# The order of k tiles and output tiles within a weight chunk of a streaming encoder step

## The reference

```
h = rms_norm(x, attn_norm[i])
y, state = even_mixer(h, ...) if i % 2 == 0 else odd_mixer(h, ...)   # h @ w_in, two attentions, concat @ w_out
x = x + y
h = rms_norm(x, mlp_norm[i])
x = x + square(relu(h @ w_up[i])) @ w_down[i]
```

## Time and profile before

| | |
|---|---|
| time, median of 3 runs | 2524.15 us (2524.02 to 2524.26) |
| span of the profiled execution, first to last instruction | 2521.4 us |
| TensorE busy, matmuls | 2514.2 us, 19,196 matmuls |
| VectorE busy | 1356.5 us |
| ScalarE busy | 998.4 us |
| DMA | 439.10 MB, mean 174 GB/s |
| granted TensorE clock, mean | 1.000 |

### The profile page before, as it was taken

One profiled execution on the slowest core, in us unless ns is written; L12 is line 12 of the kernel. 1 busy time (PEld: TensorE's weight loads), 2 busy tenths in 40 slices (PEclk: granted clock), 3 DMA queues, 4 the chain that ended last, 5 costly groups with the idle time before them and its releaser, 6 DMA issues.

```text
span 2521.4 us, 46114 instructions
## 1 busy us (share of the span) xinstructions
PE 2514.2 (100%) x19196; PEld 2487.2 (99%) x19196; DVE 1356.5 (54%) x1647; ACT 998.4 (40%) x1285; POOL 63.4 (3%) x104
## 2 busy tenths in 40 slices
PE   9999999999999999999999999999999999999999
PEld 9999999999999999999999999999999999999999
DVE  6487776544554454455544564765544544544543
ACT  5344445333333333334433455453333333333332
POOL 0002120000000000000000000000000000000000
PEclk9999999999999999999999999999999999999999
DMA  6554665444444444444444556544444444444454
GB/s 238 180 186 163 217 195 201 160 167 167 167 166 163 166 167 167 168 167 164 163 167 167 180 178 210 207 168 167 166 164 166 166 167 167 167 164 165 165 181 149
DMA packets 118525, 439.10 MB, mean 174 GB/s; under 512 B 14051, under 2 KB 14309, under 8 KB 116037
## 3 DMA queue, kind: packets, MB, share of 16 engines
q1 hardware_dynamic: 109728, 398.77, 45.3%
q0 software_dynamic: 6304, 30.94, 3.6%
q10 hardware_dynamic: 2308, 6.64, 0.9%
HBM read 426.04 MB, written 10.19 MB: 173 GB/s over the span
## 4 chain that ended last, share of the span: by engine, by line
PE 99%; DVE 0%; DMA 0%; issue 0%; ACT 0%; DVEq 0%; ACTq 0%; POOLq 0%
PE ps L425 29%; PE ps L427 29%; PE ps L426 28%; PE ps L391 3%; PE ps L393 3%; PE ps L392 3%; PE ps L579 1%; PE ps L622 1%; PE ps L453 0%; PE ps L455 0%; PE ps L454 0%; PE ps L623 0%; PE ps L525 0%; PE ps L637 0%; PE ps L774 0%; PE ps L593 0%
## 5 line engine op out<-in xcount | busy, mean ns | idle before, releaser
L839 ACT CAST w_high<-raw 128x1024 fp32r<-128x1024 f32 x755 | 787.0, 1045 | 942.4 <-PE ps L427 916.4
L1206 DVE TENSOR_TENSOR w_low<-raw,w_high 128x1024 fp32r<-128x1024 f32 x755 | 906.5, 1217 | 448.9 <-ACT w_high L839 425.5
L425 PE MATMUL ps<-x_parts,w_high 128*128 128x288 f32 x3408 | 1012.7, 297 | 0.0
L426 PE MATMUL ps<-x_parts,w_high 128*128 128x288 f32 x3408 | 1002.6, 294 | 0.0
L427 PE MATMUL ps<-x_parts,w_low 128*128 128x288 f32 x3408 | 1001.2, 294 | 0.0
L426 PEld LDWEIGHTS ps<-x_parts,w_high 128*128 128x128 f32 x3408 | 643.3, 189 | 0.2
L425 PEld LDWEIGHTS ps<-x_parts,w_high 128*128 128x128 f32 x3408 | 638.2, 187 | 5.4 <-issue 3.3
L427 PEld LDWEIGHTS ps<-x_parts,w_low 128*128 128x128 f32 x3408 | 642.5, 189 | 0.0
L425 PE MATMUL ps<-hid_parts_a,w_high 128*128 128x288 f32 x1024 | 302.3, 295 | 0.0
L426 PE MATMUL ps<-hid_low_b,w_high 128*128 128x288 f32 x1024 | 302.3, 295 | 0.0
L427 PE MATMUL ps<-hid_high_b,w_low 128*128 128x288 f32 x1024 | 302.3, 295 | 0.0
(11 more groups left out here) (330 smaller groups left out, 1818.5 us busy)
## 6 DMA issues: line engine op xcount, KB each, us to landing
raw<-in_w SPq DMA_DIRECT2D x755, 512.0 KB, 3.2
tmp<-norm_rows ACTq DMA_DIRECT2D x6, 576.0 KB, 4.3
proj<-norm_rows ACTq DMA_DIRECT2D x4, 576.0 KB, 5.0
scr<-in_k_past_B POOLq DMA_DIRECT2D x2, 1024.0 KB, 5.5
scr<-in_v_past_B POOLq DMA_DIRECT2D x2, 1024.0 KB, 7.5
scr<-in_k_past_C POOLq DMA_DIRECT2D x2, 1024.0 KB, 6.4
scr<-in_v_past_C POOLq DMA_DIRECT2D x2, 1024.0 KB, 8.3
scr<-in_k_past_D POOLq DMA_DIRECT2D x2, 1024.0 KB, 5.2
```

The lines of the kernel that those rows point to most:

```text
L425: pe.matmul(out, wh, high, start=k == 0, stop=end and apart)
L426: pe.matmul(out_low, wh, low, start=k == 0 and apart, stop=False)
L839: act.copy(used(n, w_high[:, c % HB, :]), used(n, raw[:, c % RB, :])).then_inc(high_ready, 1)
L1206: dve.tensor_tensor(used(n, w_low[:, c % RB, :]), used(n, raw[:, c % RB, :]), used(n, w_high[:, c % HB, :]).bitcast(F32), ALU.subtract)\
```

## The change

Within a chunk the loops over k tiles and output tiles change places, in both functions that hold the large products. The matmuls, their slices, their operands and their number stay. Only the order of the eight triples is another. `start` and `stop`, which mark the first and last matmul of an accumulation, still go by k.

```diff
@@ out_pair
-                    for k2 in range(CK):
-                        k = 8 * half + CK * i + k2
-                        high, low = HID(k)
-                        for f in range(GF):
+                    for f in range(GF):
+                        for k2 in range(CK):
+                            k = 8 * half + CK * i + k2
+                            high, low = HID(k)
                             at = (k2 * GF + f) * P
                             out = ps[:, 2 * (e % 2) + f, 0:T]
                             wh = w_high[:, c % HB, at:at + P]
@@ group
-                    for k2 in range(CK):
-                        k = kk * CK + k2
-                        high, low = moving(k)
-                        for f in range(tiles):
+                    for f in range(tiles):
+                        for k2 in range(CK):
+                            k = kk * CK + k2
+                            high, low = moving(k)
                             at = (k2 * GF + f) * P
                             out = ps[0:rows, 2 * odd + f, 0:T]
                             wh = w_high[:, c % HB, at:at + rows]
```

## The result

The changed kernel takes 2528.05 us (median of 21 runs, 2527.46 to 2529.27) against 2524.07 us of the kernel before in the same sessions (21 runs, 2523.34 to 2525.34). The ratio is 1.0016 with a 95% interval of 1.001 to 1.0022: 4 us slower, little, but clear of 1. It lies inside the predicted 2506 to 2536 us and within the 0.2% that the prediction called no change; the forecast of no difference at all was wrong all the same.

The account below looks back on a forecast made before the run. TensorE was taken as the bound, the time being the sum of matmul start-to-start distances. Span 2521.4 us + 0 for the change, with the median 2.75 us above the span, gave 2524 us; range 2506 to 2536 us.

Parts of the forecast that it names:

- the bank: PSUM output bank: six fewer bank changes per chunk give at most 1.3 us in all, 2523 us; no separate chance given.
- Evenness: Triple times in one chunk: odd k tile with second output tile 0.405 us, others 0.393; reordering gives 0, -17.9 or +17.9 us.
- The nearest row for the new order: One-tile group, already in the new order: its first four triples take 1.57 us, as in a full chunk, so 0 us.
- two other mechanisms: Extra triple cost in the chunks disappears, 2506 us (faster, chance 0.26), or spreads to four second-tile slices, 2542 us (slower, 0.18).
- the 2.75 us for start and end: Program start and end: the runs' median, 2524.15 us, lies 2.75 us above the profiled span.
- the surcharge: Some 12 ns extra, twice per chunk, on triples of an odd k tile and the second output tile.
- the weight slice: Reading that the extra 12 ns belongs to the data a triple reads, so the new order moves and keeps it: 0 us.
- the neighbour: Reading that the extra 12 ns comes from following the same k tile in the other bank, so it goes: 17.9 us less.
- the prediction's sign of being right: In chunks after the change, triples of 0.40 to 0.41 us still stand where odd k tiles meet the second output tile.
- the slower side: Rival: the extra 12 ns spreads to all four second-tile slices of each chunk, 18 us more, 2542 us; chance 0.18.
- the stride through the weights: Weight loads: a second-tile slice is dear when loaded after one two slices back; 18 us more, chance 0.18.
- The rule on the two read ports: TensorE weight loads: they don't slow the running matmul, distance estimated at 122.5 ns, so no order can matter; 2524 us.

Follow-up runs that it names:

- experiment 2: The changed kernel with each chunk's k tiles taken as 0, 2, 1, 3 for each output tile: 2523.55 us, ratio 0.9999 to the kernel before.
- experiment 1: Changed order everywhere but on `hid_high_b` and `hid_low_b`: 2523.51 us; changed order on those chunks alone: 2527.92 us; ratios 1.0000 and 1.0017 to the kernel before.
- experiment 3: The changed kernel with each chunk's weight slices laid out in the changed order by the host: 2527.80 us, ratio 1.0016 to the kernel before.

## Why the prediction was right or wrong

**Right: what bounds the kernel and what can't move.** TensorE is the bound, no wait and no transfer changed, the clock stayed, and the bank had no price (experiment 2 keeps one bank for 12 matmuls and costs nothing). "If I am right, an up quarter still takes about 101.5 us" held: 101.59. Two small readings beside it are off and carry nothing: the first tile is complete 9 matmuls sooner, not 12 (after 12 of the last chunk's 24 matmuls in place of 21), and after the change no triple at all follows one of the same k tile in the other bank.

**Wrong: the step "Evenness" with its neighbour "The nearest row for the new order".** The term of the sum that failed is their 0 for the new order, where the traces show 4.2 us. They priced all 744 chunks from one chunk on `x_parts` and one group on `x_parts`. That the result still lies inside the wide range is no merit of this step: the range was drawn for two other mechanisms. For the 584 chunks on `x_parts` and `hid_parts_a` 0 is what experiment 1 measured. The other 160, and the chunk behind them, were never looked at by themselves. The hint stood in the rows used: 132.5 ns in a down quarter and 132.2 in an up quarter, with the same instructions. The prediction quoted both and asked nothing; two windows more would have shown 3.17, 3.17, 3.19, 3.19. A down group in the kernel after costs 3.21 + 3.18 + 3.19 + 3.20 = 12.78 us against 12.72; 64 x 0.06 = 3.8 us.

**Wrong in size, without effect: the 2.75 us for start and end.** The 2.75 us joins the span of one execution to the median of others. Wherever the record has both for one execution, the time lies 1.74 to 1.87 us above the span. From that I estimate some 2523.2 us for the profiled execution before, 0.9 us under the median. The forecast is untouched, since the sum ends at the measured median.

**Wrong: what the surcharge belongs to.** The prediction saw two triples of 0.40 to 0.41 us per chunk and gave two readings, the weight slice or the neighbour. Neither holds. The L425 starts of one up chunk after the change:

```profile
650.42 0.29 PE L425 MATMUL ps<-x_parts,w_high 128*128 128x288 f32 x1
...
650.81 0.30 PE L425 MATMUL ps<-x_parts,w_high 128*128 128x288 f32 x1
...
651.21 0.30 PE L425 MATMUL ps<-x_parts,w_high 128*128 128x288 f32 x1
...
651.61 0.29 PE L425 MATMUL ps<-x_parts,w_high 128*128 128x288 f32 x1
...
652.00 0.29 PE L425 MATMUL ps<-x_parts,w_high 128*128 128x288 f32 x1
...
652.40 0.30 PE L425 MATMUL ps<-x_parts,w_high 128*128 128x288 f32 x1
...
652.79 0.30 PE L425 MATMUL ps<-x_parts,w_high 128*128 128x288 f32 x1
...
653.20 0.29 PE L425 MATMUL ps<-x_parts,w_high 128*128 128x288 f32 x1
...
653.59 0.29 PE L425 MATMUL ps<-x_parts,w_high 128*128 128x288 f32 x1
```

The triples take 0.39, 0.40, 0.40, 0.39, 0.40, 0.39, 0.41, 0.39 us. It is the same rhythm with a period of four triples, one place earlier in this chunk: the two dear ones are now the second and third (0.80 us together) and the sixth and seventh (0.80), where in the earlier trace rows they are the third and fourth (0.80) and the seventh and eighth (0.80). The third is now k tile 2 of the first output tile. So the dear triples are not those of odd k tiles on the second output tile, as the prediction's sign of being right had it; the rhythm follows neither slices nor output tiles here, and a chunk is 3.17 us either way. What sets the rhythm is open. An unevenness that comes back with a period needn't belong to the data that it falls on.

**Half right: the slower side.** Slower was given 0.18, with the stride through the weights as its mechanism; experiment 3 refutes that mechanism, so the direction came true by luck, for another reason. The cost of what was found, 13 ns on 160 chunks (2.1 us) and the rest in the chunks behind them, is far from the 18 us that the rival was priced at, because four fifths of the chunks have the other layout.

**The rule on the two read ports.** By the Trainium skill, "TensorE: Matmul & The Clock Gate", section "Part 2: What happens when you issue a matmul", loading the next weights doesn't slow the running matmul. That no order can matter was the prediction's own inference from it. The same section of the Trainium skill calls N/2.4 + 2.5 ns the distance of isolated matmuls and gives others for a stream in which each matmul loads its weights, as here; the prediction left that out. Its estimate of 122.5 ns is under every row here, and the starts of the moving tiles moved the distance between 132.2 and 133.3 ns; here the measurement decides.

**Open.** Why the pattern of starts has a price, and why these prices, no run says. Per chunk: aab repeated, 3.173 us; runs of 12, 3.180 on average (a quarter at 101.65, 0.10 us over 101.55 on 16 chunks); runs of 6, 3.187; runs of 3, 3.200; alternation, 3.200. From 12 to 6 to 3 the surplus about doubles with the number of changes, some 3.3 ns for each; alternation and aab don't fit that. Open too is the 3.21 us of the first chunk back on `hid_parts_a`, with which the change's price is paid for the larger part: by the matmul starts it comes each time after runs of 3, and in only 2 of 65 cases after alternation, in either of the two kernels that alternate. Of the 5.0 us between the two profiled spans, 0.8 lies outside the sum of 4.2 and was not traced; single executions of either kernel lie up to 2 us apart, and the medians differ by 4.0.

## What to carry to other kernels

Before a change to a loop is priced from one stretch, check each operand layout that passes through it: two stretches with the same instructions and another rate, here 132.5 and 132.2 ns, are a question to be answered first. Where TensorE is full, look at where moving tiles start in the partition; here putting the high and low part side by side made the loop order free and took 2 us off the kernel before. And whether a rhythm in the trace belongs to the data that it falls on shows only when the data are reordered: see whether it follows them.

## What the runs showed of the hardware that was not expected

The distance between matmuls of 288 columns in float32r on full weights depends in these runs on the sequence of start addresses of the moving tiles by their remainder modulo 256 bytes: 132.2 ns (3.173 us per 24) for two starts in the pattern aab, 133.3 ns (3.200 us) for alternation or runs of three. All starts compared lie a multiple of 128 bytes apart, and only this length of tile, 1152 bytes, was tried. Two kernels with different orders and layouts but one sequence of starts agree to 0.01 us in a stretch of 768 matmuls. The bank of PSUM, the address of the weights and the change to another moving tile have no price that these runs could show.
